# A hybrid decoder step on one core: every engine's loops written out in sequence, with waits on constants

## What is computed

```python
xn   = rmsnorm(x)
P    = xn @ w_in                        # 1024 -> 3328 columns, two head groups
# group A: RWKV-7 time mixing (8 heads x 64)
z    = p_cur + (token_shift(p_cur) - p_cur) * mu_shift
S    = S * decay + (S @ a) b^T + v k^T  # delta-rule state, one step a token
y_a  = groupnorm(S @ r) + bonus, gated
# group B: short gated convolution
y_b  = gate_b * causal_dwconv3(gate_c * h_in)
x   += concat(y_a, y_b) @ w_out
x   += cross_attention(rmsnorm(x), memory of 256 tokens) @ wo
u, g = split(causal_dwconv3(rmsnorm(x) @ w_up))     # 2 x 2816 columns
x   += (silu(g) * u) @ w_down
return rmsnorm(x), ..., the new states
```

## Time and profile before

| | |
|---|---|
| time, median of 3 runs | 4668.04 us (4664.06 to 4675.13) |
| the profiled execution | 4675.23 us, span 4673.3 us |
| mean granted TensorE clock | 0.894 of full speed |
| PE busy | 4070.5 us (87%) |
| DVE busy | 2050.8 us (44%) |
| ACT, POOL busy | 1329.6 us, 1337.2 us (28%, 29%) |
| memory traffic | 304.88 MB, 65 GB/s on average |

### The profile page before, as it was taken

The page is one execution under the profiler, slowest core; times in us unless marked ns, Lnnn a source line. Parts: engine busy times, 40 slices in busy tenths (PEclk is TensorE's granted clock), DMA queues, the critical chain, the costliest instruction groups (busy, mean ns, idle before and its releaser), DMA issues.

```text
span 4673.3 us, 83566 instructions
## 1 busy us (share of the span) xinstructions
PE 4070.5 (87%) x30117; PEld 3343.1 (72%) x30117; DVE 2050.8 (44%) x3977; ACT 1329.6 (28%) x2346; POOL 1337.2 (29%) x1107
## 2 busy tenths in 40 slices
PE   3797888998888889997989889997989696999996
PEld 3577766887678667885778667885878473878885
DVE  1234434555354535445253445445154535255554
ACT  1332233333332233333322233333322121022222
POOL 6231022444231114442320224441221020123331
PEclk9897798999888889998987989998988797699997
DMA  2320122332210213332210222331210122212221
GB/s 73 112 77 3 38 63 72 97 96 76 83 53 3 64 41 99 94 98 73 77 33 12 72 66 83 94 94 61 65 33 3 37 76 77 86 59 72 72 67 55
DMA packets 453831, 304.88 MB, mean 65 GB/s; under 512 B 17884, under 2 KB 420134, under 8 KB 452942
## 3 DMA queue, kind: packets, MB, share of 16 engines
q1 hardware_dynamic: 453606, 301.67, 21.3%
HBM read 288.61 MB, written 13.23 MB: 65 GB/s over the span
## 4 chain that ended last, share of the span: by engine, by line
PE 69%; DVE 14%; issue 9%; ACT 3%; POOL 3%; DMA 1%; DVEq 1%; POOLq 0%; ACTq 0%; SPq 0%
PE psum L624 68%; DVE xlo L1415 2%; POOL wlo L541 2%; PE psum L628 1%; DVE shifted L1415 1%; DVE zr L1418 1%; ACT whi L1085 1%; DVE xT L1415 1%; DVE shifted L1418 1%; DVE kkn_y L1415 1%; POOL stage L483 1%; DMA out_y_prompt<-zr 1%; DVE xT L1418 1%; ACT stage L1085 0%; DVE stage L1415 0%
## 5 line engine op out<-in xcount | busy, mean ns | idle before, releaser
L541 POOL TENSOR_TENSOR wlo<-wraw,whi 128x1024 fp32r<-128x1024 f32 x480 | 1152.3, 2401 | 2750.0 <-ACT whi L1085 2750.0
L624 PE MATMUL psum<-xhi,whi 128*128 128x512 f32 (+1 forms) x3136 | 1252.4, 399 | 52.7 <-DVE xlo L1415 37.7
L624 PE MATMUL psum<-xhi,wlo 128*128 128x512 f32 (+1 forms) x3136 | 1222.6, 390 | 0.0
L624 PE MATMUL psum<-xlo,whi 128*128 128x512 f32 (+1 forms) x3136 | 1222.0, 390 | 0.0
L1085 ACT ACTIVATE whi<-wraw 128x1024 fp32r<-128x1024 f32 x480 | 507.4, 1057 | 1219.0 <-PE psum L624 1152.7
L624 PEld LDWEIGHTS psum<-xhi,whi 128*128 128x128 f32 x3136 | 598.6, 191 | 224.4 <-issue 51.6
L624 PEld LDWEIGHTS psum<-xhi,wlo 128*128 128x128 f32 x3136 | 598.2, 191 | 124.7
L624 PEld LDWEIGHTS psum<-xlo,whi 128*128 128x128 f32 x3136 | 600.5, 191 | 113.1 <-issue 1.4
L1415 DVE TENSOR_TENSOR xT<-xT,psum 128x512 f32<-128x512 f32 (+1 forms) x416 | 286.1, 688 | 232.3 <-PE psum L624 160.4
L1725 DVE TENSOR_SCALAR zr<-zr,fcw 128x512 f32<-128x512 f32 x176 | 91.5, 520 | 587.7 <-POOL fcarry L578 586.3
L624 PE MATMUL psum<-hhi,whi 128*128 128x512 f32 x704 | 280.6, 399 | 23.3 <-DVE hlo L1415 19.0
(11 more groups left out here) (269 smaller groups left out, 4999.0 us busy)
## 6 DMA issues: line engine op xcount, KB each, us to landing
wraw<-in_w_up SPq DMA_DIRECT2D x176, 512.0 KB, 3.8
wraw<-in_w_in SPq DMA_DIRECT2D x104, 512.0 KB, 3.8
wraw<-in_w_down SPq DMA_DIRECT2D x88, 512.0 KB, 3.3
wraw<-in_w_out SPq DMA_DIRECT2D x32, 512.0 KB, 3.9
wraw<-in_wq SPq DMA_DIRECT2D x32, 512.0 KB, 3.8
wraw<-in_wo SPq DMA_DIRECT2D x32, 512.0 KB, 3.8
kkn_y<-in_x_prompt SPq DMA_DIRECT2D x4, 2048.0 KB, 8.3
out_y_prompt<-zr SPq DMA_DIRECT2D x16, 512.0 KB, 2.7
```

The costliest lines, as they stand in the source:

```text
L541: return e.tensor_tensor(wlo[i][:, :, :], wraw[i][:, :, :], whi[i][:, :, :].bitcast(F32), ALU.subtract).then_inc(lo_ready[i], 1)
L624: return e.matmul(out, lhsT, rhs, start=start, stop=stop)
```

## The change

Every loop on every engine becomes a loop of the program that writes the kernel: the body is emitted as often as it ran. The turn number is then a plain number, so every address and every value waited for is a constant. The counter loses its turns and the table `LOOPS`, and the increments of the four `passed` semaphores are taken out. No operation on data is added, removed or put in another order, and the same semaphores are waited for, at the same places. Cut to its core (each of the 25 loops and of the `passed` increments goes like those shown):

```diff
 class Counts:
-    def __init__(self, eng, name, passed=None):
-        self.eng, self.name, self.passed, self.n, self.turns = eng, name, passed, {}, []
+    def __init__(self):
+        self.n = {}
 
     def __call__(self, sem, k=1):
         v = self.n[sem.name] = self.n.get(sem.name, 0) + k
-        for i, per in self.turns:
-            if per.get(sem.name):
-                v = i * per[sem.name] + v
         return v
-    @contextmanager
-    def loop(self, label, count):
...
-        if self.passed is not None and self.turns:
-            self.eng.sem_inc(self.passed, 1)
-        with self.eng.Fori(0, count) as i:
-            self.turns.append((i, per))
-            yield i
-            self.turns.pop()
...
             def carries(a, tile):
                 e.wait_ge(eb_ready[a], c(eb_ready[a]))
-                e.sem_inc(passedG, 1)
                 e.tensor_copy(eb[:, a, 0:2], fcarry[:, bass.ds(tile, 1), :].rearrange("p a b -> p (a b)")).then_inc(gch, 1)
                 e.wait_ge(gch, c(gch))
-                e.sem_inc(passedG, 1)
                 e.tensor_copy(fcarry[:, bass.ds(tile, 1), :].rearrange("p a b -> p (a b)"),
                               eb[:, a, TB:TB + 2]).then_inc(eb_carry[a], 1)
...
                 operands(1, C, True)
-                with c.loop("wkv", NC // 2 - 1) as j:
+                for j in range(NC // 2 - 1):
                     operands(0, j * (2 * C) + 2 * C)
...
                 ffn_up(s, tuple(range(KT)))
-                with c.loop("ffn" + "s" * last, NF // 2 - 1):
+                for _ in range(NF // 2 - 1):
                     ffn_up(s)
                     ffn_down(s)
                 ffn_down(s)
```

More of the change, by code:

```diff
@@ L385, in one_block @@
             def one_block(b, last):
-                with c.loop("in", NIN // 2 - 1) as i:
+                for i in range(NIN // 2 - 1):
                     for j in range(2):
@@ L401, in one_block @@
                 ffn_up(0)
-                with c.loop("ffn", NF // 2 - 1) as i:
+                for i in range(NF // 2 - 1):
                     ffn_up(i + 1)
@@ L544, in splits @@
             def splits(label, pairs):
-                with c.loop(label, pairs):
+                for _ in range(pairs):
                     split(0)
@@ L661, in phase @@
                 if pairs > 1:
-                    with c.loop(label + "s" * bool(sample), pairs - 1):
+                    for _ in range(pairs - 1):
                         dense(0, 0, sample, None, n)
@@ L919, in one_block @@
                 head_rows(8)
-                with c.loop("gates" + "s" * last, 4):
+                for _ in range(4):
                     dense(0, 0, s)
@@ L1121, in _ @@
                 split_x(k, NMEM)
-            with c.loop("mem", 8):
+            for _ in range(8):
                 for j in range(2):
@@ L1241, in one_block @@
                     split_x(k)
-                with c.loop("shift", NRW // 2) as i:
+                for i in range(NRW // 2):
                     for j in range(2):
@@ L1282, in one_block @@
                         split_w(j)
-                with c.loop("h_in", 2):
+                for _ in range(2):
                     for j in range(2):
@@ L1338, in one_block @@
                 ffn_hidden()
-                with c.loop("ffn" + "s" * last, NF // 2 - 1) as i:
+                for i in range(NF // 2 - 1):
                     ffn_up(i + 1)
@@ L1542, in _ @@
             lo(before, NMEM)
-            with c.loop("mem", 8) as i:
+            for i in range(8):
                 for j in range(2):
@@ L1628, in residual @@
                 acc_start()
-                with c.loop(label + "s" * last, KT // 2) as i:
+                for i in range(KT // 2):
                     for j in range(2):
@@ L1814, in sample_out @@
                         e.sem_inc(free[4 + j], 1)
-                with c.loop("shift" + "s" * last, NRW // 2) as i:
+                for i in range(NRW // 2):
                     for j in range(2):
@@ L1863, in one_block @@
                     e.wait_ge(vch, c(vch))
-                with c.loop("gate_c" + "s" * last, 2) as i:
+                for i in range(2):
                     for j in range(2):
@@ L1868, in one_block @@
                 e.wait_ge(a2v, c(a2v, 4))
-                with c.loop("h_in" + "s" * last, 2) as i:
+                for i in range(2):
                     for j in range(2):
@@ L1962, in one_block @@
                 normalise("norm_x")
-                with c.loop("q" + "s" * last, KT // 2) as i:
+                for i in range(KT // 2):
                     for j in range(2):
```

116 lines of the change are left out of this document (12 added, 104 removed).

## The result

The changed kernel took 4522.26 us (median of 4 runs, 4500.34 to 4529.23) against 4666.38 us before: a ratio of 0.9666 with a 95% interval of 0.9644 to 0.9689, so 3.3% or about 144 us faster. The span of the profiled execution is 4519.4 us, 153.9 us less than before; that of the kernel before was 9 us slower than its median, this one was 1 us faster than its own.

A forecast was written before the change was run, and what follows sets the result against it. PE was taken to bound the kernel (69% of the chain), with gains only where it waits for other engines. Terms A to E, 12 + 9 + 9 + 12 + 4 = 46 us, took 4668 to 4622 us, range 4600 to 4662.

The forecast's parts named there:

- E: The recurrence: register rows and signals lost on DVE, ACT, POOL, mostly covered by PE; 4 us, bounds -12 and +16.
- The prediction's own sign of being wrong: Wrong if the four recurrences together differ by more than 15 us; they were expected at 158 to 168 us.
- A: Feed-forward turns, blocks 0 to 2: PE's 0.38 us wait on POOL closes; 12 us with first turns, bounds 0 and 15.
- B: Last block's feed-forward turn with sample tokens: PE's two waits on DVE go nearly whole; 9 us, bounds 3 and 13.
- C: Ends of feed-forward stages and projections: DVE's gaps close while PE is done; 9 us, bounds 3 and 13.
- D: Between input projection and recurrence, and token-shift loop's end: DVE's gaps ahead of PE close; 12 us, bounds 4 and 16.
- Fetching the longer program: Rival: PE's longer code, up to 126 more blocks, stalls PE; up to 190 us lost, 4812 us; chance 0.10.
- More than counted: Rival: DVE's lag sets more recurrence levels, E gives 16 us, other terms upper bounds; 73 us, 4595 us; chance 0.12.

The follow-up runs named there:

- others_only: Kernel before with the loops of DVE, ACT, POOL and SP written out, PE's loops and all `passed` increments kept: 4634.86 us, ratio 0.9907.
- pe_loops_no_signals: Changed kernel with PE's loops left as loops, other engines written out and all `passed` increments out: 4517.95 us, ratio 0.9657.
- after: The changed kernel itself, with the whole change against the kernel before: 4522.26 us, ratio 0.9666.
- out_keep_passedP: Changed kernel with only PE's `passedP` increments put back ahead of their matmul groups: 4628.56 us, ratio 0.9892.

## Why the prediction was wrong

**E, the step that failed.** The prediction set "a signal per level" beside the register rows and let PE's own work cover both: 1 us a block, 4 in all, bounds -12 and +16. The recurrences gained 120 us. Three things were wrong in it. The signal that mattered stands on PE, the engine that sets the end there; the step named DVE, ACT and POOL and said of PE only that its program "was in sequence here before". The change took 240 increments a block out of PE's own program (211 sequencer instructions a block, since some shared one with a wait that stays), and that part of the diff had no price: put back alone, they cost 105 us in the recurrences (533 to 638). The register rows of the other engines were not covered either: with PE's increments gone, writing out the recurrence's loops and leaving out `passedV` gave another 56 us (601 to 545). And the clock was booked as scatter ("may change which stretch is slow"), while 85 of the 120 us came as PE's busy time at a higher granted clock. The rows were there: two recurrences with the same work lie 9 us apart at mean clocks of 0.78 and 0.83, and the 1.51 us stop was read only as a rival's price, never as time that the change might give back. The prediction's own sign of being wrong came: the four recurrences differ by 120 us, not by at most 15.

**A was right.** 11.4 us were counted for the turns of blocks 0 to 2. In the kernel after, almost the whole feed-forward loop of block 1 is one piece of the chain: 1344 matmuls in 304.99 us, 0.2269 us each, nearly the 0.2265 of the earlier trace rows:

```profile
1765.14 304.99 PE psum L532 x1344
```

At a block's first turn PE waits 1.00 us instead of 1.17, near the fifth that was counted. The dependent pair of DVE operations takes the same 1.54 us in a turn as outside, as forecast.

**B was right.** A turn of the last block was to fall from 44.62 to about 43.7 us. Two of DVE's rows one turn apart are 43.72 us apart:

```profile
4232.93 0.17 DVE L1308 TENSOR_TENSOR sw<-sw 128x16 f32<-128x16 f32 x1
...
4276.65 0.17 DVE L1308 TENSOR_TENSOR sw<-sw 128x16 f32<-128x16 f32 x1
```

**C was too large.** At the end of the feed-forward stage the adds did close up, but PE still starts 10.72 us after the first of them instead of 10.30, since a product after them took 1.82 us instead of 0.76. The chain of the kernel after, and POOL's split at the time:

```profile
2076.58 0.70 DVE xT L1308
...
2083.25 1.82 DVE stage L1308
...
2087.30 4.87 PE psum L532 x12
```

```profile
2082.17 2.34 POOL L455 TENSOR_TENSOR wlo<-wraw,whi 128x1024 fp32r<-128x1024 f32 x1 [1.66 <-ACT whi L986]
```

What the 5 us that C counted for the output projections came to is not shown.

**D was too large.** 2.1 us a block were counted ahead of the recurrence. The wait went from 13.52 to 12.98 us. DVE's timeline in the kernel after, against the earlier trace rows, and POOL's split at the same place before and after:

```profile
1335.36 0.69 DVE L1308 TENSOR_TENSOR ws<-ws,psum 128x512 f32<-128x512 f32 x1
1336.20 2.22 DVE L1769 TENSOR_SCALAR shifted<-ws,par 128x512 f32<-128x512 f32 x1
...
1340.87 0.17 DVE L1778 COPY ccarry<-ws 128x8 f32<-128x8 f32 x1
```

```profile
1368.38 2.35 POOL L541 TENSOR_TENSOR wlo<-wraw,whi 128x1024 fp32r<-128x1024 f32 x1 [2.94 <-ACT whi L1085]
```

```profile
1335.78 2.35 POOL L455 TENSOR_TENSOR wlo<-wraw,whi 128x1024 fp32r<-128x1024 f32 x1 [3.04 <-ACT whi L986]
```

The gaps between the operations have gone, but the tile takes 5.51 us instead of 5.43: the same TENSOR_SCALAR took 2.22 us instead of 1.46. In both kernels this operation starts while POOL's split runs and ends 0.29 us after it (at 1371.02 and 1370.73 before, at 1338.42 and 1338.13 after). In C, too, the product that took longer ends 0.56 us after POOL's split in both kernels (at 2155.46 and 2154.90 before, at 2085.07 and 2084.51 after). So the rows read as if these operations could not end ahead of POOL's split, and starting them earlier gained nothing. The step took DVE's durations as fixed and moved only the gaps. At the end of the token-shift loop PE's wait fell from 1.2 to 0.9 us, not by 0.9.

```profile
PEld psum L532 <- DVEq L1727: 0.9, 1, 0.9
```

A to D together still came to 34 us of the 42 between the two profiled executions, some 10 of which is that they lie apart by more than the medians; `others_only`, which has A to D nearly alone, gained some 45, 5 of them in the recurrences.

**The rivals.** Fetching the longer program did not happen: the blocks rose from 167 to 238, and the stops fell. The stops that this rival went by were real, and as counted above they lie at the edges of code blocks, but the length of the program was not their cause: `pe_loops_no_signals` has 164 blocks and `after` 238, with recurrences of 532 and 533 us, while `out_keep_passedP` has the long program and the stops. The Trainium skill, Runtime: NRT & Kernel Launch, Instruction fetch mechanics, holds that crossing a block is mostly hidden; the kernel after agrees (no stop at such an edge in its recurrences), the kernel before with 23.4 us of them does not. The branches of PE's loops, which that section calls expensive, cost nothing that these runs show. *More than counted* named the right place, the recurrence, with the wrong engine and a bound of 16 us.

## What to carry to other kernels

Price every line that a change takes out of the engine that sets the end, signals and waits included; "nobody waits for it" is no price of zero, and here 960 unread increments on PE, taken out alone, gave some 57 us (0.9877), and put back alone took some 105 of the 144 us away (0.9892 against 0.9666). Where a stage shows two clocks, ask first what idles the engine inside it: in the recurrences 35 us came as closed stops and 85 us as PE's busy time at a higher clock. And gaps between operations are not all gain, since an operation that moves can start under another engine's and take longer, as 2.22 us for 1.46 beside POOL's split here.

## What was not expected of the hardware

The increments made by PE's sequencer, 240 in a recurrence, cost some 75 us beyond the waits that they held (4629 against 4557 us), with stops of up to 2.3 us that have no releaser and lie at the edges of code blocks. Two causes add up to more than their sum: 14 and 52 us of the recurrences alone, 108 together (with `passedV` gone as well). And loops that an engine runs itself were free on PE, whose branch took up to 0.2 us each: 4518 us with its loops, 4522 without. The branch's row in the kernel before, by the line of the loop helper (columns: engine's sequencer, operation, count, duration in ns as least, median and most, first and last start in us):

```profile
L143 PEldq COMPARE_BRANCH  x123: 76/208/235, 91.4 to 4595.1; - x123
```
